# Input norm's scale moved onto the weights, key projection in larger pieces, operand addresses rounded to 512 bytes

## What is computed

```python
h = _rmsnorm(x, norm_g[l])          # x * rsqrt(mean(x*x) + EPS) * norm_g
proj = jnp.einsum('bsd,de->bse', h, w_in[l])
xa, ga, q, ckv, gb, qi, ki, wi = jnp.split(proj, IN_SPLITS, axis=-1)
...
y = jnp.concatenate([ya, yb], axis=-1)
x = x + jnp.einsum('bse,ed->bsd', y, w_out[l])
return _rmsnorm(x, final_norm_g)
```

## Time and profile before

| | |
|---|---|
| runs before | 1635.7, 1634.93, 1634.05 us |
| the profiled execution | 1632.13 us |
| its span, first to last instruction | 1630.4 us |
| TensorE matmul busy | 1583.4 us, 97% of the span |
| VectorE busy | 854.6 us, 52% |
| ScalarE busy | 579.6 us, 36% |
| GpSimd busy | 431.6 us, 26% |

### The profile page before, as it was taken

The page is one execution under the profiler, slowest core; times in us unless marked ns, Lnnn a source line. Parts: engine busy times, 40 slices in busy tenths (PEclk is TensorE's granted clock), DMA queues, the critical chain, the costliest instruction groups (busy, mean ns, idle before and its releaser), DMA issues.

```text
span 1630.4 us, 21469 instructions
## 1 busy us (share of the span) xinstructions
PE 1583.4 (97%) x7547; PEld 1319.6 (81%) x7547; DVE 854.6 (52%) x1498; ACT 579.6 (36%) x845; POOL 431.6 (26%) x289
## 2 busy tenths in 40 slices
PE   6999999999999999999999999999998899999998
PEld 6788999888888888888888888777776788888886
DVE  6427555577777787875555555276777100031003
ACT  6335555433444444331111111355555222232320
POOL 2212222222222222222222222110010444444650
PEclk9999999999999999999999999999999999999999
DMA  7212111122222112233222221321222522237322
GB/s 261 87 46 78 40 45 39 32 55 62 61 61 61 42 52 68 68 86 102 71 77 71 77 71 57 105 85 61 67 79 75 222 95 99 94 103 297 132 85 103
DMA packets 132310, 141.36 MB, mean 87 GB/s; under 512 B 8518, under 2 KB 103848, under 8 KB 129960
## 3 DMA queue, kind: packets, MB, share of 16 engines
q1 hardware_dynamic: 130728, 136.55, 26.2%
q0 software_dynamic: 1536, 4.20, 0.8%
HBM read 116.08 MB, written 24.64 MB: 86 GB/s over the span
## 4 chain that ended last, share of the span: by engine, by line
PE 84%; issue 8%; DVE 4%; ACT 2%; DMA 1%; POOL 1%; DVEq 0%; SPq 0%; ACTq 0%; POOLq 0%
PE ps L1036 17%; PE ps L1037 17%; PE ps L1038 17%; PE ps L1313 6%; PE ps L1312 6%; PE ps L1314 6%; PE ps L1253 2%; PE ps L1139 2%; PE ps L1141 2%; PE ps L1217 2%; PE ps L1230 1%; PE ps L1338 1%; PE ps L1337 1%; PE ps L1339 1%; DMA w_raw<-in_w_in 1%
## 5 line engine op out<-in xcount | busy, mean ns | idle before, releaser
L1036 PE MATMUL ps<-hT_hi,w_lo 128*128 128x512 f32 (+1 forms) x1344 | 511.4, 380 | 2.8 <-POOL w_lo L662 2.8
L1037 PE MATMUL ps<-hT_lo,w_hi 128*128 128x512 f32 (+1 forms) x1344 | 509.2, 379 | 0.0
L1038 PE MATMUL ps<-hT_hi,w_hi 128*128 128x512 f32 (+1 forms) x1344 | 509.2, 379 | 0.0
L662 POOL TENSOR_TENSOR w_lo<-w_raw,w_hi 128x512 fp32r<-128x512 f32 x168 | 240.6, 1435 | 757.1 <-ACT w_hi L742 757.1
L1036 PEld LDWEIGHTS ps<-hT_hi,w_lo 128*128 128x128 f32 x1344 | 252.3, 188 | 48.4 <-issue 5.2
L1037 PEld LDWEIGHTS ps<-hT_lo,w_hi 128*128 128x128 f32 x1344 | 252.4, 188 | 43.3 <-issue 0.2
L1038 PEld LDWEIGHTS ps<-hT_hi,w_hi 128*128 128x128 f32 x1344 | 252.3, 188 | 42.6
L742 ACT ACTIVATE w_hi<-w_raw 128x512 fp32r<-128x512 f32 x168 | 104.8, 630 | 479.0 <-PE ps L1038 472.7
L1312 PE MATMUL ps<-wo_hi,hT_lo 128*128 128x512 f32 x448 | 174.4, 389 | 3.1 <-DVE hT_lo L1581 3.1
L1640 DVE TENSOR_TENSOR res<-ps,res 128x512 f32<-128x512 f32 x32 | 21.8, 691 | 294.2 <-PE ps L1314 243.8
L1313 PE MATMUL ps<-wo_lo,hT_hi 128*128 128x512 f32 x448 | 174.3, 389 | 0.0
(11 more groups left out here) (188 smaller groups left out, 1821.4 us busy)
## 6 DMA issues: line engine op xcount, KB each, us to landing
w_raw<-in_w_in SPq DMA_DIRECT2D x168, 256.0 KB, 2.9
wo_raw<-in_w_out SPq DMA_DIRECT2D x64, 512.0 KB, 3.6
xin<-in_x SPq DMA_DIRECT2D x8, 1024.0 KB, 5.0
res<-in_x SPq DMA_DIRECT2D x8, 1024.0 KB, 9.4
...
```

The costliest lines, as they stand in the source:

```text
L662: nc.gpsimd.tensor_tensor(w_lo[:, j, :, :], w_raw[:, j, :, :], w_hi[:, j, :, :].bitcast(F32), ALU.subtract).then_inc(w_lo_s, 1)
L1036: nc.tensor.matmul(o, wlo, hi, start=(kt == 0), stop=False)
L1037: nc.tensor.matmul(o, whi, lo, start=False, stop=False)
L1038: return nc.tensor.matmul(o, whi, hi, start=False, stop=(kt == KT - 1))
```

## The change

The norm's scale leaves the tokens and goes onto the rows of the weights. `norm_g` is loaded as 16 rows of 128, the first DMA of SyncE's queue, transposed by TensorE and copied by VectorE to `g_col` (128 x 16). `norm_x` multiplies by the reciprocal root alone, with one tensor as input. GpSimd multiplies each piece of `w_raw` in place by `g_col`, broadcast along the columns (`gain`), before ScalarE makes `w_hi` of it; `high` waits for GpSimd (`w_g_s`) in place of the DMA. The ring of token blocks has four buffers. `keys_tokens` runs for 256 tokens after blocks 2 and 4 are transposed, in place of 128 tokens four times. The weights of `T_C` are fetched ahead of the last two token blocks. The small tensors now stand in front of `hT_hi`, with padding, so that it begins at 16,896 = 33 x 512; others are reordered or share the room of `wk_hi` (1024 bytes), and `kw_hi` and `kw_lo` have rows of 96 columns.

The diff, cut to its core (new semaphores and lines that don't matter are left out):

```diff
--- before.py
+++ after.py
@@ -59,8 +59,7 @@
 
 PARS = (CONV + 4) * G + CT + 2
 
-XB = 3
-FIRST_HALF = NT // P
+XB = 4
 AHEAD = 3
 
 FIRST_SCORED = TOPK // P
@@ -138,23 +137,29 @@
 
 
         sb = alloc(ctx)
+        eps = sb("eps", [P, 1])
+        pause = sb("pause", [P, 1])
+        stat = sb("stat", [P, 16])
+        sums = sb("sums", [P, QB, 3])
+        g_col = sb("g_col", [P, KT])
+        sb("line_pad", [P, 24])
         hT_hi = sb("hT_hi", [P, KT, S], F32R)
         hT_lo = sb("hT_lo", [P, KT, S], F32R)
         ident = sb("ident", [P, P])
         causal = sb("causal", [P, P])
-        par_t = sb("par_t", [P, PARS])
+
+        pw = ExitStack()
+        sW = alloc(pw)
+        w_nat = sW("w_nat", [P, QB, IH])
+        par_t = sW("par_t", [P, PARS + 4])
         conv_w = par_t[:, 0:CONV * G].rearrange("p (j g) -> p j g", g=G)
         lru_p = par_t[:, CONV * G:(CONV + 4) * G].rearrange("p (k g) -> p k g", g=G)
         c_g = par_t[:, PARS - 4:PARS - 2]
         k_gb = par_t[0:ID, PARS - 2:PARS]
-        decay = sb("decay", [P, 2, G])
-        sp_t = sb("sp_t", [P, 5, G])
-        eps = sb("eps", [P, 1])
-        pause = sb("pause", [P, 1])
-        stat = sb("stat", [P, 3 * XB])
-        w_nat = sb("w_nat", [P, QB, IH])
-        sums = sb("sums", [P, QB, 3])
-        sb("line_pad", [P, 8])
+        decay = sW("decay", [P, 2, G])
+        sp_t = sW("sp_t", [P, 5, G])
+        pw.close()
+        wk_hi = sb("wk_hi", [P, CT, HD], F32R)
 
 
         ph = ExitStack()
@@ -166,15 +171,15 @@
         p0 = ExitStack()
         s0 = alloc(p0)
         xin = s0("xin", [P, XB, D])
-        kw_hi = s0("kw_hi", [P, KT, KW], F32R)
-        kw_lo = s0("kw_lo", [P, KT, KW], F32R)
+        kw_hi = s0("kw_hi", [P, KT, 96], F32R)[:, :, 0:KW]
+        kw_lo = s0("kw_lo", [P, KT, 96], F32R)[:, :, 0:KW]
...
-        g_bc = s0("g_bc", [P, D])
+        g_rows = s0("g_rows", [KT, P])
         onehot = s0("onehot", [BUCKETS, BR])
+        bias_sb = s0("bias_sb", [NH * COPIES, BR])
+        rel_wide = s0("rel_wide", [BUCKETS, NH, COPIES])
         rel = s0("rel", [BUCKETS, NH])
-        rel_wide = s0("rel_wide", [BUCKETS, NH, COPIES])
-        bias_sb = s0("bias_sb", [NH * COPIES, BR])
         p0.close()
         scores = sbp("scores", [P, SCORED])
 
...
-        top8 = sC("top8", [P, QB, 8])
         wg_hi = sC("wg_hi", [P, 2, P], F32R)
         wg_lo = sC("wg_lo", [P, 2, P], F32R)
+        top8 = sC("top8", [P, QB, 8])
...
-        wk_hi = s3("wk_hi", [P, CT, HD], F32R)
...
@@ -439,18 +447,17 @@
                 sp.wait_ge(x_tp, 2 * (i - XB) + 2)
                 sp.dma_start(xin[:, i % XB, :], x[i * P:(i + 1) * P, :]).then_inc(x_rest[i - XB], 16)
 
+            sp.dma_start(g_rows[:, :], a["norm_g"][0].rearrange("(k p) -> k p", p=P)).then_inc(g_in, 16)
             x_load(0)
-            sp.dma_start(g_bc[:, :], a["norm_g"].broadcast_to([P, D])).then_inc(g_in, 16)
             x_load(1)
             weights(T_KW, COL_KI, KW)
             for i in range(2, XB):
                 x_load(i)
             x_next(XB)
             x_next(XB + 1)
+            weights(T_C, COL_CKV)
             x_next(XB + 2)
-            weights(T_C, COL_CKV)
             x_next(XB + 3)
-            x_next(XB + 4)
 
             sp.dma_start(rel[:, :], a["rel_bias"]).then_inc(bias_in, 16)
             sp.dma_start(onehot[:, :], a["onehot"]).then_inc(bias_in, 16)
@@ -645,21 +652,37 @@
                                     base=0, pattern=[[-1, P]], channel_multiplier=1).then_inc(consts, 1)
 
 
+            def gain(j, n):
+
+                return g_col[:, j * PK:(j + 1) * PK].rearrange("p (k o) -> p k o", o=1).broadcast_to([P, PK, n])
+
+            def scale_kw(j):
+                pool.wait_ge(w_in_s[j], 16)
+                part = w_raw[:, j, :, 0:KW]
+                nc.gpsimd.tensor_tensor(part, part, gain(j, KW), ALU.mult).then_inc(kw_g_s, 1)
+
             def cut_kw(j):
                 part = slice(j * PK, (j + 1) * PK)
-                pool.wait_ge(w_in_s[j], 16)
+                pool.wait_ge(kw_g_s, j + 1)
                 nc.gpsimd.tensor_copy(kw_hi[:, part, :], w_raw[:, j, :, 0:KW]).then_inc(w_hi_s, 1)
                 pool.wait_ge(w_hi_s, j + 1)
                 nc.gpsimd.tensor_tensor(kw_lo[:, part, :], w_raw[:, j, :, 0:KW], kw_hi[:, part, :].bitcast(F32),
                                         ALU.subtract).then_inc(w_lo_s, 1)
 
+            pool.wait_ge(g_made, 1)
+            scale_kw(0)
             for j in range(PIECES):
+                if j + 1 < PIECES:
+                    scale_kw(j + 1)
                 cut_kw(j)
 
             def low(t):
                 for j in range(PIECES):
+                    part = w_raw[:, j, :, :]
+                    pool.wait_ge(w_in_s[j], 16 * t + 16)
+                    nc.gpsimd.tensor_tensor(part, part, gain(j, P), ALU.mult).then_inc(w_g_s, 1)
                     pool.wait_ge(w_hi_s, 4 * t + j + 1)
-                    nc.gpsimd.tensor_tensor(w_lo[:, j, :, :], w_raw[:, j, :, :], w_hi[:, j, :, :].bitcast(F32), ALU.subtract
+                    nc.gpsimd.tensor_tensor(w_lo[:, j, :, :], part, w_hi[:, j, :, :].bitcast(F32), ALU.subtract
                                             ).then_inc(w_lo_s, 1)
 
             with pool.Fori(1, TILES) as t:
@@ -737,7 +760,7 @@
             def high(t, js=range(PIECES)):
 
                 for j in js:
-                    act.wait_ge(w_in_s[j], 16 * t + 16)
+                    act.wait_ge(w_g_s, 4 * t + j - 3)
                     act.wait_ge(w_used, 4 * t + j + 1)
                     nc.scalar.activation(w_hi[:, j, :, :], w_raw[:, j, :, :], ACT.Copy).then_inc(w_hi_s, 1)
 
@@ -754,11 +777,11 @@
                 if i + 2 < QB:
                     square(i + 2)
                     root_x(i + 2)
-                if FIRST_HALF <= i:
-                    high(1, [i - FIRST_HALF])
+                if XB <= i:
+                    high(1, [i - XB])
 
             act.wait_ge(small_tp, 1)
-            nc.scalar.activation(par_t[:, :], X[1][:, 0:PARS], ACT.Copy).then_inc(small_cp, 1)
+            nc.scalar.activation(par_t[:, 0:PARS], X[1][:, 0:PARS], ACT.Copy).then_inc(small_cp, 1)
             act.wait_ge(bias_mm, 1)
             nc.scalar.activation(bias_sb[:, :], X[0][:, 0:BR], ACT.Copy).then_inc(bias_cp, 1)
             act.wait_ge(kw_used, 1)
@@ -1027,6 +1050,9 @@
             nc.tensor.sem_inc(ro_mm, 4)
 
             pe.wait_ge(id_made, 1)
+            pe.wait_ge(g_in, 16)
+            nc.tensor.transpose(X[0][:, 0:KT], g_rows[:, :], ident[0:KT, 0:KT]).then_inc(g_tp, 1)
+            pe.wait_ge(g_made, 1)
 
             def triple(o, j, k, tok):
 
@@ -1078,11 +1104,11 @@
             for i in range(QB):
                 if i + 1 < QB:
                     turn_x(i + 1)
-                if i < FIRST_HALF:
+                if i in (1, 3):
                     pe.wait_ge(h_lo, 2 * i + 2)
-                    keys_tokens(i * P, P)
-                else:
-                    project_tile(T_C, 1, 0, parts=ALL_TOKENS[:1], js=[i - FIRST_HALF], last_part=False)
+                    keys_tokens((i - 1) * P, 2 * P)
+                elif i > 3:
+                    project_tile(T_C, 1, 0, parts=ALL_TOKENS[:1], js=[i - 4], last_part=False)
             pe.wait_ge(h_lo, 2 * QB)
             keys_tokens(NT, NT).then_inc(kw_used, 1)
             pe.wait_ge(small_in, 16 * 8)
@@ -1363,14 +1389,15 @@
 
             nc.vector.memset(eps[:, :], EPS).then_inc(eps_made, 1)
             nc.vector.memset(par_rows[:, :], 0.0).then_inc(rows_clear, 1)
-            dve.wait_ge(g_in, 16)
+            dve.wait_ge(g_tp, 1)
+            nc.vector.tensor_copy(g_col[:, :], X[0][:, 0:KT]).then_inc(g_made, 1)
 
             def norm_x(i):
                 dve.wait_ge(x_sd, i + 1)
                 root, inverse = (stat[:, k * XB + i % XB:k * XB + i % XB + 1] for k in (1, 2))
                 chain(nc.vector.reciprocal(inverse, root))
-                stt(xin[:, i % XB, :], xin[:, i % XB, :], inverse, g_bc[:, :], ALU.mult, ALU.mult
-                    ).then_inc(x_norm, 1)
+                nc.vector.tensor_scalar(xin[:, i % XB, :], xin[:, i % XB, :], inverse, None, ALU.mult
+                                        ).then_inc(x_norm, 1)
 
             def low_x(i):
                 for j in range(2):
@@ -1390,6 +1417,7 @@
             nc.vector.tensor_copy(rel_wide[:, :, :], rel[:, :].rearrange("b (h o) -> b h o", o=1).broadcast_to(
                 [BUCKETS, NH, COPIES])).then_inc(rel_made, 1)
             dve.wait_ge(x_tp, 2 * QB)
+            dve.wait_ge(rel_made, 1)
             chain(nc.vector.memset(ones_k[:, :], 1.0 / ID))
             nc.vector.memset(ones_c[:, :], 1.0 / C).then_inc(ones_made, 1)
             chain(nc.vector.memset(scores[:, :], 0.0))
```

More of the change, by code:

```diff
@@ L308, in layer @@
         g_in = sem("g_in")
+        g_tp = sem("g_tp")
+        g_made = sem("g_made")
         rel_made = sem("rel_made")
```

2 lines of the change are left out of this document (added).

## The result

The changed kernel takes 1636.72 us, the median of 16 executions (1634.17 to 1638.45), beside 1633.86 us for the kernel before (16 executions): a ratio of 1.0021, 95% interval 1.0014 to 1.0027. It is slower by 2.9 us, where a gain of 4.5 us was forecast. The profiled execution took 1634.17 us, span 1632.5.

What follows compares the result with a forecast made beforehand. TensorE, with a matmul at work in 97% of the span, was taken as the bound. The front's -5.5 us and +1.0 for GpSimd's hold on VectorE gave -4.5: 1634.93 to 1630.4 us, range 1624 to 1641.

Steps and rivals of the forecast that it cites:

- The front: Stretch up to the last keys: earlier start, larger key pieces and fewer tile 1 waits, 5.5 us less, bounds -9 and -2.
- The keys' term: Keys in pieces of 256 tokens: 2.5 us less matmul time against new transpose waits, net 0.9 less, bounds 0.3 and 2.5.
- The two other terms, -2.6 and -2.0: Start of the front, without the 1 MB DMA and with a shorter norm: -2.6 us; tile 1's waits for `w_lo`: -2.0.
- The addresses: Operands of TensorE's fp32r matmuls placed at multiples of 512: taken as 0, bounds -74 us and a few us up.
- the main case: The prediction's own case: whole kernel at 1630.4 us, range 1625 to 1633, addresses doing nothing; chance 0.56.
- Rival 1: Addresses count in TensorE's matmuls: the fixed 13.3 ns go, 74 us less, 1556, or some 1570; chance 0.10.
- The step that failed: GpSimd's 168 scales, 235 us more work, fit into its idle time and don't reach TensorE: nothing.
- the cover: In the indexer stage, over 16 us before a piece's use and 2.6 us a piece hide ScalarE's wait for GpSimd.
- GpSimd's hold on VectorE: At the indexer tiles' borders and first tile, the two engines hold each other up: +1.0 us, bounds 0 and 10.4.
- Rival 2: Slower by GpSimd's lock on VectorE at the indexer tiles' borders and first tile: +5, 1640; chance 0.16.
- Rival 3: Front's gain fails as ScalarE takes 4.8 us a block: under 3 us, less 1 to 2 of lock, 1634; chance 0.18.

Runs made afterwards that it cites:

- e9: e6 with 124 waits on a long-met condition put on TensorE's queue, only to move the code behind them; 1626.32 us, ratio 0.9955 to the kernel before.
- e7: Changed kernel with GpSimd's four scales ahead of its four differences at every weight tile but tile 5; ratio 0.9978 to the kernel before.
- e8: Changed kernel with GpSimd's scales left out of the computation, keys still in pieces of 256; ratio 0.9971 to the kernel before.
- e5: Changed kernel with GpSimd's four scales ahead of its four differences at weight tile 4 alone; ratio 0.9977 to the kernel before.
- e1: Changed kernel with GpSimd's four scales ahead of its four differences at every weight tile; ratio 0.9991 to the kernel before.
- e10: Changed kernel with the keys of the first four token tiles in pieces of 128 again; ratio 1.0025 to the kernel before.
- e2: e1 with 32 more words of padding, so TensorE's operands lie 128 bytes above a multiple of 512; ratio 0.9990 to the kernel before.
- e3: e1 with the keys of the first four token tiles in pieces of 128 again; ratio 0.9986 to the kernel before.
- e6: e5 with the keys of the first four token tiles in pieces of 128 again; 1629.05 us, ratio 0.9979 to the kernel before.
- e4: Kernel before with the keys of the first four token tiles in pieces of 256 and nothing else; ratio 0.9994 to the kernel before.

## Why the prediction was wrong

**The front** as a whole went nearly as forecast. Norm 1.29 us for the 1.4 expected; second transposes at 14.71 for 14; gain 3.8 us for 5.5, within its bounds of 2 to 9. The keys' term was missized: the pitch was right (0.114 for 0.120), the waits between transposes were not (1.3 to 2 us expected, 3.2 measured between e9 and e7), so that -0.9 should have been about +0.9, outside its bounds. The two other terms, -2.6 and -2.0, came out at -4.6 together in e9. Their parts didn't: TensorE's waits for `w_lo` fell by 0.8 us in the change, where 2.0 was expected to go. And a part of the front's gain is luck of the clock in the one execution that was profiled: e8 has the same front but for the scales and gained 2.4.

**The addresses** did nothing, as the main case had it. Rival 1 falls.

**The step that failed** is the one that costed the 168 scales at nothing, because "ScalarE's `high`, which now waits for GpSimd, waits for TensorE anyway, and the piece it makes is used three pieces (over 16 us) later". The first half is not so: at 41 of the 168 pieces it was GpSimd's scale that ScalarE waited for last. The second half, the cover, held for all of these but the three of tile 4 (TensorE busy in 369.00 of 369 us, with 29 of them in it; e5 keeps 38 of them and loses nothing by them). At tile 4 ScalarE comes from the keys' chain, TensorE's condition is long met, and `high` waits for GpSimd, whose next scale stands behind a `low` that waits for `high`. The step also looked at when the piece is used and not at what stands behind `high` on ScalarE: the exponentials and the stacks that the first score matmul waits for. It cost 6.1 us, with 1.8 us of lower clock behind it. e5 takes the order away at that tile alone and the wait goes; e8, without scales, has the same 0.95 us.

**GpSimd's hold on VectorE**, +1.0 with bounds of 0 and 10.4, measured 1.5 in e5 (two of 0.8), and 2.3 more in e1; the term was right in kind and within its bounds. Rival 2 had the right place, the borders of the indexer, and nearly the right time (1640), but the wrong cause: the change loses by an order on a queue. Rival 3 did not come; the last keys started before 59.

**Not foreseen at all:** 2.6 us won at the start of attention, 1.2 of them by where the code happened to lie and 1.4 because the clock did not fall behind the shorter wait. Without them the change would end at +4.7 in the profiled execution. e10 does not win them: it is 1.4 us ahead of the change at 156 us and 1.5 behind it at 1052. So that the change lost only 2.9 us in the median owes something to luck.

## What to carry to other kernels

When an engine is put between a load and its consumer, write out its queue and look at what the new instruction stands behind. A producer behind a wait for its own consumer turns two overlapping streams into turns. The turns alone need not cost anything, as at 38 of the 41 pieces here; the place to look is the one tile where the consumer comes late and its next work is waited for. And a part of a microsecond that moves in the front may be won or lost a thousand microseconds later, at a wait that is set by a transfer: compare variants at the same instruction in both traces, not by the total, and look first whether the clock came up at the same instruction.

## What the runs showed beside

- TensorE's granted clock fell for some microseconds behind waits (at tile 4 to 0.50 to 0.74 in windows of four and five us), and the wait's length alone doesn't say when. At tile 4 it fell behind 3.1 to 7.0 us (the change, e1, e2, e3, e10) and not behind 0.95; at the first wait of attention behind 3.10 to 3.25 (before, e3, e10) and not behind 3.00 (e6) or 1.9 to 2.1; in the front behind 2.9 and 3.0 in e1 and e5, and not behind 2.95 in e4 (at 52 us). Further on all thirteen traces have the same waits: behind the one of 2.5 us near 1250 it fell in seven of them, behind the one of 3.35 us near 1270 in ten (not in before, after and e4). There is one trace of each kernel, so whether the kernel or the execution decides is open. A wait may cost more than its length: the 6.1 us at tile 4 came with 1.8 more.
- An in-place multiplication by a broadcast column took GpSimd 1.04 us for 128 x 512, less than the difference of two tensors of that size (1.29).
- Whether an instruction load falls among other transfers moved a wait by 1.1 us, in kernels whose work was the same.
